# Two-layer hybrid block with routed experts: gate stores halved and doubled in number, part of them issued past the stage boundary, row products dealt out anew

## The chip, the cores and the metric

The kernel runs on one core of one Trainium2 chip. The metric is the time of one execution on the device, in microseconds, as the median of several executions. TensorE does the matrix products, VectorE, ScalarE and GpSimd the rest, and 16 DMA engines move data between the large memory (HBM) and the on-chip buffer (SBUF). The profile calls the engines PE, DVE, ACT and POOL; SP is the engine that only issues transfers.

## The reference, cut to what matters

Two layers, each of three parts: a mixer, an attention over a memory of 256 rows, and a feed-forward part with 16384 small experts. The change lies in the third, apart from the renaming of two semaphores. There, 512 tokens of width 1024 each choose 16 experts in each of 8 heads, 128 in all:

```python
idx = top 16 of the 16 x 16 sums of two top-16 lists, per head   # 8 heads
gate = softmax(best_v)
h = gelu(einsum('ted,td->te', expert_u[it], xt))
out = einsum('te,ted->td', gt * h, expert_v[it])
```

## The kernel before, in words

**Tiling of the expert part.** The 512 tokens are four tiles of 128 (token tile 0 to 3). Token tile 0 goes by gathered rows: for each of its 128 selections GpSimd fetches one expert row per token by an indirect transfer (128 x 1024 f32, 512 KiB), VectorE multiplies it with the token and sums it (`dots`, L1794), and in the last stage it fetches rows of the second expert table and adds them (`add_row`, L1928). Token tiles 1 to 3 (384 tokens) go densely, through all 128 blocks of 128 experts, and their gates are spread out into a dense table `gates` of 128 x 128 x 384 in HBM.

**First stage.** A loop over 128 slots j, one for each expert block. In a slot SP loads one weight tile of 512 KiB (L82, `load_tile`), ACT splits off its high half (L89) and DVE the low half (L95), PE does 24 matmuls of 128x384 (L116 to L118), ACT takes the gelu of them (L1677, `hidden`), and SP stores that result of 192 KiB (`keep`, L1516). Four f32 tiles (`wf`) and four split tiles (`wh`, `wl`) stand in rings of four. The split for slot j + 4 is what ACT does right after the gelu of slot j, and DVE right after that: the DVE part of slot j begins with the L95 of tile j + 4. The load of tile j + 7 is issued by SP right after the store of the hidden result of slot j.

Beside that run three identical rounds of 36 slots, one for each of token tiles 1 to 3, after 4 slots at the start: 20 slots of selection (`choose`, 16 calls over 20 slots, each with VectorE's top-16 instructions, every second one with a second search), 4 slots of picking, 4 slots in between, 8 slots of spreading (two `chunk` calls each; PE L1617/L1618, ACT L1715 copies them into the buffer `stage`). So spreading takes slots 32 to 39, 68 to 75 and 104 to 111. Slots 112 to 127 are the last stretch. The 128 row products of token tile 0 are dealt out over the slots by the planner `dots_of_slot`, in proportion to a room that `dots_by` estimates from `other_work`.

**Gate stores.** When a token tile is spread, `keep` stores its gates from `stage` to HBM (L1522), 8 stores of 1 MiB, one in each of the first 8 slots that follow (40 to 47, 76 to 83, 112 to 119), in runs of 512 bytes. In SP's program a store stands between the hidden store of slot j and the load of tile j + 7.

**Second stage.** Again 128 blocks: SP loads the expert's second tile (512 KiB) and reads the hidden result and the gates of that block (192 KiB each, L1533 and L1534), DVE multiplies them, ACT and DVE split the product, PE does 24 matmuls of 128x384 (L1635 to L1637). GpSimd gathers one row per block into `vrow`, which lies in the memory of `stage`, as does the sum `acc`. The start of this stage waits for the last gate store in three places: SP before its first block, GpSimd before the first gather (L1737), and DVE before it clears `acc` (L1935, L1936).

The order on each engine is the program order: every engine runs its own list, and semaphores tie them. SP's list and GpSimd's list hold their waits in order too. Of HBM transfers, those of SP form one queue (q1), the indirect ones of GpSimd another (q0).

Of the kernel before, what the change touches and what calls it, by code (L numbers as in the profile page):

```python
# [15 lines left out]
P = 128  # L16
D, SEQ, DEPTH = 1024, 512, 2
KT, NT = D // P, SEQ // P
# [8 lines left out]
EB = PK  # L27
# [22 lines left out]
RING = 4  # L50
# [344 lines left out]
def ssm_parameters(m, dve, step, par, v, c, cc, b, lag):  # L395

    nc = m.nc
    lr, li = par[:, PAR["lam_re"]], par[:, PAR["lam_im"]]
    TT, OP = nc.vector.tensor_tensor, ALU
    dve.wait_ge(m.ssm_trig, 1)  # L400
    step(TT(v.are, v.r, v.cos, OP.mult))
    step(TT(v.aim, v.r, v.sin, OP.mult))
    step(TT(v.r2, v.r, v.r, OP.mult))
    step(nc.vector.tensor_scalar(v.re, v.are, -1.0, None, OP.add))
    step(TT(v.t0, lr, lr, OP.mult))
    step(TT(v.t1, li, li, OP.mult))
    step(TT(v.t0, v.t0, v.t1, OP.add))
    step(nc.vector.reciprocal(v.inv, v.t0))
    step(TT(v.t0, v.re, lr, OP.mult))
    step(TT(v.t1, v.aim, li, OP.mult))  # L410
    step(TT(v.t0, v.t0, v.t1, OP.add))
    step(TT(v.fre, v.t0, v.inv, OP.mult))
    step(TT(v.t0, v.aim, lr, OP.mult))
    step(TT(v.t1, v.re, li, OP.mult))
    step(TT(v.t0, v.t0, v.t1, OP.subtract))
    step(TT(v.fim, v.t0, v.inv, OP.mult))
    dve.wait_ge(m.weights, 16 * N_SMALL)
    wide = [P, ST, 2 * SC]
    fre, fim = (x.unsqueeze(2).to_broadcast(wide) for x in (v.fre, v.fim))
    t = v.wide  # L420
    step(TT(t[:, 0], c[:, 0], fre, OP.mult))
    step(TT(t[:, 1], c[:, 1], fim, OP.mult))
    step(TT(cc[:, 0], t[:, 0], t[:, 1], OP.subtract))
    step(TT(t[:, 0], c[:, 0], fim, OP.mult))
    step(TT(t[:, 1], c[:, 1], fre, OP.mult))
    step(nc.vector.scalar_tensor_tensor(cc[:, 1], t[:, 0], -1.0, t[:, 1], OP.mult, OP.subtract))
    are, aim = (x.unsqueeze(2).to_broadcast(wide) for x in (v.are, v.aim))
    step(TT(t[:, 0], b[:, 0], are, OP.mult))
    step(TT(t[:, 1], b[:, 1], aim, OP.mult))
    step(TT(lag[:, 0], t[:, 0], t[:, 1], OP.subtract))  # L430
    step(TT(t[:, 0], b[:, 0], aim, OP.mult))
    step(TT(t[:, 1], b[:, 1], are, OP.mult))
    step(TT(lag[:, 1], t[:, 0], t[:, 1], OP.add))
    dve.sem_inc(m.lags, 1)
    step(TT(t[:, 0], cc[:, 0], are, OP.mult))
    step(TT(t[:, 1], cc[:, 1], aim, OP.mult))
    step(TT(cc[:, 2], t[:, 0], t[:, 1], OP.add))
    step(TT(t[:, 0], cc[:, 0], aim, OP.mult))
    step(TT(t[:, 1], cc[:, 1], are, OP.mult))
    step(TT(cc[:, 3], t[:, 1], t[:, 0], OP.subtract))  # L440
# [21 lines left out]
def mixer(nc, m, a, layer):  # L462
# [71 lines left out]
    def tensor(pe):  # L534
# [40 lines left out]
        for b in range(NT):  # L575
            pe.wait_ge(m.evac, N_IN + 6 + b - 1)
            MM(B[(N_IN + 6 + b) % 2][:, 0:MH * MV], ckv[:, 0, b * P:(b + 1) * P], ukv[:, MH * NOPE:],
               start=True, stop=True).then_inc(m.up, 1)
        pe.wait_ge(m.lags, 1)
        for z in range(2):  # L580
            pe.wait_ge(m.evac, N_IN + 10 + z - 1)
            for j in range(ST // 4):
# [4 lines left out]
        for st in range(ST):  # L587
            j, q = st // 4, st % 4
# [199 lines left out]
    def scalar(act):  # L788
# [38 lines left out]

        for i in range(13):
            if i == 6:
                act.wait_ge(m.keys_turned, 1)  # L830
                stick(0)
            act.wait_ge(m.up, i + 1)
            bank = B[(N_IN + i) % 2]
            if i < 6:
                for z in range(2):
                    last = AF((qh, kh)[i // 3][0:NOPE, 2 * (i % 3) + z, :], bank[64 * z:64 * z + 64, :], ACT.Copy)
            elif i < 10:
                last = AF(vm[:, i - 6, :], bank[:, 0:MH * MV], ACT.Copy)
            elif i < 12:
                last = AF(ab[:, i - 10], bank[:, 0:ST // 4 * P].rearrange("p (j n) -> p j n", j=ST // 4), ACT.Copy)  # L840
            else:
                last = AF(now, bank[:, 0:ST // 4 * 2 * SC].rearrange("p (j n) -> p j n", j=ST // 4), ACT.Copy)
            last.then_inc(m.evac, 1)
# [153 lines left out]
    def vector(dve):  # L997
        step = Steps(dve, m.dve_step)
        dve.sem_inc(m.split_done, 2 * RING)
        for n in range(N_IN):  # L1000
# [20 lines left out]
                STT(ml[:, :, :], memf, XS, mh[:, :, :], ALU.mult, ALU.subtract).then_inc(m.mem_low, 1)  # L1021
            if n == T_KRS + 8:
                ssm_parameters(m, dve, step, par, v, cz, cc, bs, lag)
        dve.sem_inc(m.keys_turned, 1)

        def turn_queries(r):
            dve.wait_ge(m.rot, r + 1)
# [370 lines left out]
R_PICK = 1  # L1398
# [1 line left out]
R_U = EB // RING  # L1400
ST_N = NT - 1
R_LAST = R_U - R_PICK - ST_N * R_TOK
STORES = 8
TURN = RING - 1
AHEAD = RING - 1
ND = SEQ - P
N_SEL = PH * TOP
GR = 4
HALF = TOP // 2
LATER = 2 * RING - 1  # L1410
LONG, SHORT = 4, 4
# [22 lines left out]
    return 1.3 + CPH * 2.8  # L1434


def dots_by(j):

    room = [min(1.8, max(0.0, 5.6 - other_work(i))) for i in range(EB)]
    return int(sum(room[:j]) * N_SEL / sum(room) + 0.5)  # L1440


# [5 lines left out]
def experts(nc, m, a, layer):  # L1448
# [57 lines left out]
    def sync(sp):  # L1506
        sp.wait_ge(m.mem_yl, KT)
        sp.dma_start(keys, a.keys[layer]).then_inc(m.keys_in, 16)
        with sp.Fori(0, R_PQ) as r:
            for k in range(RING):  # L1510
                load_tile(m, sp, a.proj[layer, r * RING + (T_PQ + k)], r + R_0, k)

        def keep(j):

            sp.wait_ge(m.tile_out, N_PQ + j + 1 + 2)
            sp.dma_start(m.hid[j], gst[j % RING]).then_inc(m.g_out[j % RING], 16)  # L1516
            for tt in range(1, NT):
                c = j - spread_slots(tt).stop
                if c in range(STORES):
                    i = slice(c * EB // STORES, (c + 1) * EB // STORES)  # L1520
                    sp.wait_ge(m.staged, tt * CPT + 2)
                    sp.dma_start(m.gates[i, :, (tt - 1) * P:tt * P].rearrange("i j t -> j i t"), stage[:, i, :])\  # L1522
                        .then_inc(m.gates_out, 16)

        for j in range(EB):
            if j >= LATER:
                keep(j - LATER)
            load_tile(m, sp, a.experts[layer, j], R_0 + R_PQ + j // RING, j % RING)

        def block(g, k):  # L1530
            load_tile(m, sp, a.experts[layer, g * RING + (EB + k)], g + (R_0 + R_PQ + R_U), k)
            sp.wait_ge(m.gw_used, g * RING + (k + 1))
            sp.dma_start(gw[:, k, 0, :], m.hid[g * RING + k]).then_inc(m.gw_in[k], 16)  # L1533
            sp.dma_start(gw[:, k, 1, :], m.gates[g * RING + k]).then_inc(m.gw_in[k], 16)  # L1534

        sp.wait_ge(m.gates_out, 16 * STORES * ST_N)
        for k in range(RING):
            sp.wait_ge(m.g_out[k], 16 * 2 + 1)
        for g in range(2):
            for k in range(RING):  # L1540
                if EB + g * RING + k - LATER < EB:
                    keep(EB + g * RING + k - LATER)
                block(g, k)
        for k in range(RING):
            sp.wait_ge(m.g_out[k], 16 * R_U + 1)
        with sp.Fori(2, R_U // 2) as g:
            for k in range(RING):
                block(g, k)
        sp.wait_ge(m.dots, N_SEL)
        sp.dma_start(m.xT[:, :, :], m.xsave.rearrange("p (k t) -> p k t", k=KT)).then_inc(m.x_back, 16)  # L1550
        with sp.Fori(R_U // 2, R_U) as g:
            for k in range(RING):
                block(g, k)
        for k in range(RING):
            load_tile(m, sp, a.tiles[layer * N_PROJ + (N_PROJ + k)], R_0 + R_PQ + 2 * R_U, k)
# [171 lines left out]
    def gpsimd(pool):  # L1727
# [3 lines left out]
        for i in range(N_SEL):  # L1731
            if i >= GR:
# [1 line left out]
            pool.indirect_dma_start(urow[:, i % GR, :], None, a.urows,  # L1734
                                    bass.IndirectOffsetOnAxis(ap=uidx[:, i:i + 1], axis=0))\
                .then_inc(m.u_in[i % GR], 16)
        pool.wait_ge(m.gates_out, 16 * STORES * ST_N)  # L1737
        rows = a.experts.rearrange("l e p d -> (l e p) d")
        for i in range(N_SEL):
            if i >= GR:  # L1740
# [6 lines left out]
    def vector(dve):  # L1747
# [184 lines left out]
            slot(j)  # L1932
            dots(j)
        step.restart()
        dve.wait_ge(m.gates_out, 16 * STORES * ST_N)  # L1935
        step(V.memset(acc, 0.0))  # L1936
        for k in range(RING):
            slot(EB - RING + k)
# [32 lines left out]


INPUTS = "x mem positions freq mask par proj experts urows keys uq ukv glu bz cz bs".split()
SEMAPHORES = """lags keys_turned split_done tile_used high_done params weights s_x s_small s_pool s_ang s_sin evac lat_sq lat_sum
lat_done up rot rot_done ssm_exp ssm_args ssm_trig table ssm_bu ssm_mul ssm_prod ssm_read
ssm_y sb_z sb_sp sb_t sb_w sb_wm sb_o sb_y mla_sc mla_nm mla_e mla_p mla_tr mla_pt mla_av mla_y
gelu_done glu_in glu_mm glu_sig glu_done grp_sq grp_sum y_norm yh_done yl_done
lat_sd grp_sd xh_done mem_in mem_high mem_low kv_out q_out mem_sc mem_nm mem_e mem_p mem_tr mem_pt mem_av
mem_yh mem_yl keys_in tile_out act_step dve_step pool_step scored
sc_copied best gate_e selected sel_turned sel_high hot spread  # L1980
staged gates_out gw_used multiplied prod_high prod_done out_done xtok_turned xtok_in idx_ready dots dots_gelu added
x_saved x_back second_hot""".split()


# [3 lines left out]
def program(nc, inputs, out, depth=DEPTH):  # L1988
    with ExitStack() as ctx:
        def sb(name, shape, dt=F32):  # L1990
# [7 lines left out]
        m = Named()  # L1998
        m.nc = nc
        sems = [ctx.enter_context(nc.semaphore(name)) for name in SEMAPHORES]  # L2000
        (m.lags, m.keys_turned, m.split_done, m.tile_used, m.high_done, m.params, m.weights, m.s_x, m.s_small, m.s_pool,
         m.s_ang, m.s_sin, m.evac, m.lat_sq, m.lat_sum, m.lat_done, m.up, m.rot, m.rot_done,
         m.ssm_exp, m.ssm_args, m.ssm_trig, m.table, m.ssm_bu, m.ssm_mul, m.ssm_prod, m.ssm_read,
         m.ssm_y, m.sb_z, m.sb_sp, m.sb_t, m.sb_w, m.sb_wm, m.sb_o, m.sb_y, m.mla_sc, m.mla_nm, m.mla_e,
# [2 lines left out]
         m.lat_sd, m.grp_sd, m.xh_done, m.mem_in, m.mem_high, m.mem_low, m.kv_out, m.q_out, m.mem_sc, m.mem_nm,  # L2007
         m.mem_e, m.mem_p, m.mem_tr, m.mem_pt, m.mem_av, m.mem_yh, m.mem_yl, m.keys_in, m.tile_out, m.act_step,
         m.dve_step, m.pool_step, m.scored, m.sc_copied, m.best, m.gate_e,
         m.selected, m.sel_turned, m.sel_high, m.hot, m.spread, m.staged, m.gates_out,  # L2010
         m.gw_used, m.multiplied, m.prod_high, m.prod_done, m.out_done, m.xtok_turned, m.xtok_in, m.idx_ready,
         m.dots, m.dots_gelu, m.added, m.x_saved, m.x_back, m.second_hot) = sems
        m.loaded = [ctx.enter_context(nc.semaphore(f"loaded{k}")) for k in range(RING)]
# [162 lines left out]
```

## Time and profile before

| what | value |
|---|---|
| time, median of 3 executions | 3841.4 us (3839.28 to 3844.2) |
| the profiled execution's own time | 3847.1 us |
| its span, first to last instruction | 3845.4 us |
| PE busy | 3446.5 us (90%) |
| DVE busy | 2873.0 us (75%) |
| ACT / POOL busy | 1480.1 us (38%) / 1020.2 us (27%) |
| mean granted TensorE clock | 0.954 |
| moved by DMA | 840.91 MB |

The expert part of layer 1 takes from about 705 us to about 1890 us of the span, that of layer 2 from about 2615 us. A row of the windows view gives, for one stretch, the busy time of each engine with its instructions, the granted clock of PE, the busy share of the DMA engines and the GB/s that they moved. A row of the waits view reads "engine, line, what it waited for: us in total, times, longest". A row of the timeline is start, duration, engine, line, operation, and in brackets the idle time before it with what ended it.

### The profile page before, as it was taken

To read this page: it belongs to the slowest core of one execution; us is meant where nothing else is said; L and a number is where in the kernel's file an instruction comes from. 1 tells how busy PE (TensorE), PEld (TensorE's weight loads), DVE (VectorE), ACT (ScalarE), POOL (GpSimd) and SP (SyncE) were. 2 spreads that over 40 slices of the span, in tenths; PEclk is the share of its full clock that TensorE was granted. 3 is DMA by queue.
4 is the path that set the end of the run, shared out by engine and by line. 5 is a ranking of instruction groups with operands and counts; after the bars stand their busy time and mean duration, and the time that the engine had idled before them with its cause. 6 is when DMAs were issued, how large, how long until landed. Compare 5 with 4: busy or idle time off the path is not lost.

```text
span 3845.4 us, 58583 instructions
## 1 busy us (share of the span) xinstructions
PE 3446.5 (90%) x20122; PEld 1992.1 (52%) x20122; DVE 2873.0 (75%) x5232; ACT 1480.1 (38%) x1978; POOL 1020.2 (27%) x742
## 2 busy tenths in 40 slices
PE   7899988979798889999888999889787979999997
PEld 3444644546464556666444446345454546566663
DVE  5765435898979768888847654368989896788887
ACT  4324423335353533333333244223343535333333
POOL 0510100231413134444324100002323141344442
PEclk9999998989999999999998899999998999999998
DMA  5001312586869699999540013126778786999995
GB/s 172 29 1 50 127 55 77 204 285 238 319 208 317 217 375 370 374 387 371 212 143 12 1 61 116 55 88 234 259 270 285 239 322 212 377 368 379 384 369 189
DMA packets 386162, 840.91 MB, mean 219 GB/s; under 512 B 32608, under 2 KB 231264, under 8 KB 385248
## 3 DMA queue, kind: packets, MB, share of 16 engines
q1 hardware_dynamic: 311712, 565.38, 42.0%
q0 software_dynamic: 73728, 268.47, 19.0%
q10 hardware_dynamic: 576, 5.37, 0.4%
q8 instruction: 60, 0.98, 0.1%
q14 instruction: 86, 0.70, 0.1%
HBM read 732.14 MB, written 106.95 MB: 218 GB/s over the span
## 4 chain that ended last, share of the span: by engine, by line
PE 31%; DVE 9%; DMA 3%; issue 3%; ACT 2%; SPq 2%; DVEq 0%; POOL 0%; ACTq 0%
PE ps L1635 4%; PE ps L1637 4%; PE ps L1636 4%; PE ps L116 3%; PE ps L117 3%; PE ps L118 3%; DMA wf<-experts 2%; SPq L82 2%; DVE wl L95 1%; DVE xT L1794 1%; DMA xT<-urows,small 1%; PE ps L152 1%; ACT wh L89 1%; ACT xh L181 0%; DVE small L1759 0%
## 5 line engine op out<-in xcount | busy, mean ns | idle before, releaser
L116 PE MATMUL ps<-xh,wh 128*128 128x384 f16 (+1 forms) x2880 | 1007.1, 350 | 215.2 <-DVE wl L95 62.9
L95 DVE SCALAR_TENSOR_TENSOR wl<-wf,wh 128x1024 f16<-128x1024 f32 x656 | 804.1, 1227 | 443.9 <-ACT wh L89 421.7
L89 ACT ACTIVATE wh<-wf 128x1024 f16<-128x1024 f32 x656 | 690.7, 1053 | 1025.2 <-PE ps L1637 582.3
L117 PE MATMUL ps<-xl,wh 128*128 128x384 f16 (+1 forms) x2880 | 1005.4, 349 | 0.0
L118 PE MATMUL ps<-xh,wl 128*128 128x384 f16 (+1 forms) x2880 | 1003.8, 349 | 0.0
L1734 POOL DMA_INDIRECT xT<-urows,small x256 | 363.4, 1419 | 1170.6 <-DVE xT L1794 888.6
L1635 PE MATMUL ps<-work,wh 128*128 128x384 f16 x2048 | 667.7, 326 | 6.0 <-DVE work L1919 4.3
L1637 PE MATMUL ps<-work,wl 128*128 128x384 f16 x2048 | 667.6, 326 | 0.0
L1636 PE MATMUL ps<-work,wh 128*128 128x384 f16 x2048 | 667.6, 326 | 0.0
L1742 POOL DMA_INDIRECT work<-experts,small x256 | 453.1, 1770 | 579.9 <-DVE work L1928 553.6
L116 PEld LDWEIGHTS ps<-xh,wh 128*128 128x128 f16 x2880 | 287.7, 100 | 478.0 <-ACT work L1677 104.5
L118 PEld LDWEIGHTS ps<-xh,wl 128*128 128x128 f16 x2880 | 287.7, 100 | 243.6 <-issue 20.9
L117 PEld LDWEIGHTS ps<-xl,wh 128*128 128x128 f16 x2880 | 287.5, 100 | 230.8 <-issue 19.2
L1928 DVE SCALAR_TENSOR_TENSOR work<-work,small 128x1024 f32<-128x1024 f32 x256 | 328.9, 1285 | 96.9 <-DVE work L1919 96.2
L1794 DVE SCALAR_TENSOR_TENSOR xT<-xT,work 128x1024 f32<-128x1024 f32 x256 | 308.2, 1222 | 19.8 <-DMA xT<-urows,small 12.5
L1635 PEld LDWEIGHTS ps<-work,wh 128*128 128x128 f16 x2048 | 200.4, 98 | 139.1 <-issue 5.0
L1637 PEld LDWEIGHTS ps<-work,wl 128*128 128x128 f16 x2048 | 200.4, 98 | 132.4
L1636 PEld LDWEIGHTS ps<-work,wh 128*128 128x128 f16 x2048 | 200.4, 98 | 131.4
L202 POOL TENSOR_SCALAR xT<-xT,small 128x512 f32<-128x512 f32 x24 | 51.9, 2171 | 748.2 <-ACT xh L181 748.2
L1677 ACT ACTIVATE work<-ps 128x384 f32<-128x384 f32 x192 | 93.5, 487 | 326.7 <-PE ps L118 300.9
L1715 ACT ACTIVATE work<-ps 128x1024 f32<-128x1024 f32 x96 | 184.0, 2011 | 51.6 <-PE ps L1618 51.6
L1617 PE MATMUL ps<-work,sq 128*128 128x128 f16 x768 | 114.7, 239 | 62.5 <-DVE sq L1885 62.5
(347 smaller groups left out, 4146.2 us busy)
## 6 DMA issues: line engine op xcount, KB each, us to landing
wf<-experts SPq DMA_DIRECT2D x512, 512.0 KB
wf<-proj SPq DMA_DIRECT2D x144, 512.0 KB
gates<-work SPq DMA_DIRECT2D x48, 1024.0 KB
work<-hid SPq DMA_DIRECT2D x256, 192.0 KB
work<-gates SPq DMA_DIRECT2D x256, 192.0 KB
hid<-work SPq DMA_DIRECT2D x192, 192.0 KB
hid<-small SPq DMA_DIRECT2D x64, 192.0 KB
xsave<-xT ACTq DMA_DIRECT2D x2, 2048.0 KB, 7.0
```

The source lines that it names most:

```text
L89: m.nc.scalar.activation(m.wh[:, slot, :], m.wf[:, k, :], ACT.Copy, scale=WS).then_inc(m.high_done, 1)
L95: m.nc.vector.scalar_tensor_tensor(m.wl[:, slot, :], m.wf[:, k, :], WS, m.wh[:, slot, :], ALU.mult, ALU.subtract).then_inc(m.split_done, 1)
L116: m.nc.tensor.matmul(out, wh[:, k, :], xh[:, k, 0:n], start=(k == order[0]), stop=False)
L117: m.nc.tensor.matmul(out, wh[:, k, :], xl[:, k, 0:n], start=False, stop=False)
L118: last = m.nc.tensor.matmul(out, wl[:, k, :], xh[:, k, 0:n], start=False, stop=(k == order[-1]))
L1635: MM(out, m.wh[:, k, c], ph[:, k, :], start=first, stop=False)
L1636: MM(out, m.wh[:, k, c], pl[:, k, :], start=False, stop=False)
L1637: done = MM(out, m.wl[:, k, c], ph[:, k, :], start=False, stop=last)
L1734: pool.indirect_dma_start(urow[:, i % GR, :], None, a.urows, bass.IndirectOffsetOnAxis(ap=uidx[:, i:i + 1], axis=0))\
L1742: pool.indirect_dma_start(vrow[:, i % GR, :], None, rows, bass.IndirectOffsetOnAxis(ap=vidx[:, i:i + 1], axis=0))\
L1794: STT(row, row, 1.0, xtok, ALU.mult, ALU.mult, accum_out=hd[:, i:i + 1]).then_inc(m.dots, 1)
L1928: STT(acc, row, wd[:, bass.ds(i, 1)], acc, ALU.mult, ALU.add).then_inc(m.added, 1)
```

## The change

- `STORES` is 16 in place of 8: each gate store has 512 KiB (8 of the 128 first-key columns), one in each of the 16 slots after a spreading.
- `HEAD` is 5, the number of stores that free the memory of `vrow` and `acc`. The first five stores of the last token tile count on a semaphore of their own, `gates_head`.
- `keep` runs seven slots behind SP's loads, so that the last seven stores of the last token tile now stand in SP's program among the first blocks of the second stage. SP waits there for the two earlier token tiles and for the five; it waits for all stores before its third group of four blocks. GpSimd and DVE wait for the five alone.
- The planner `dots_by` gives a storing slot a room of at most 1.1, any other at most 1.9 (1.8 before for all).
- Two semaphores, `lags` and `keys_turned`, become one, `prepared`, waited for at 1 and at 2. DVE raises them in that order before and after.

```diff
-    dve.sem_inc(m.lags, 1)
+    dve.sem_inc(m.prepared, 1)
...
-        pe.wait_ge(m.lags, 1)
+        pe.wait_ge(m.prepared, 1)
...
-                act.wait_ge(m.keys_turned, 1)
+                act.wait_ge(m.prepared, 2)
...
-        dve.sem_inc(m.keys_turned, 1)
+        dve.sem_inc(m.prepared, 1)
...
-STORES = 8
+GR = 4
+STORES = 16
+HEAD = -(-STORES * (GR + 1) * D // (EB * P))
...
+def storing(j):
+
+    at = j - R_PICK * RING
+    return at >= R_TOK * RING and at % (R_TOK * RING) < STORES
...
-    room = [min(1.8, max(0.0, 5.6 - other_work(i))) for i in range(EB)]
+    room = [min(1.1 if storing(i) else 1.9, max(0.0, 5.6 - other_work(i))) for i in range(EB)]
...
+                    done = m.gates_head if tt == NT - 1 and c < HEAD else m.gates_out
                     sp.dma_start(m.gates[i, :, (tt - 1) * P:tt * P].rearrange("i j t -> j i t"), stage[:, i, :])\
-                        .then_inc(m.gates_out, 16)
+                        .then_inc(done, 16)
...
-        sp.wait_ge(m.gates_out, 16 * STORES * ST_N)
+        sp.wait_ge(m.gates_out, 16 * STORES * (ST_N - 1))
+        sp.wait_ge(m.gates_head, 16 * HEAD)
         for k in range(RING):
             sp.wait_ge(m.g_out[k], 16 * 2 + 1)
         for g in range(2):
...
                 block(g, k)
+        sp.wait_ge(m.gates_out, 16 * (STORES * ST_N - HEAD))
         for k in range(RING):
             sp.wait_ge(m.g_out[k], 16 * R_U + 1)
...
-        pool.wait_ge(m.gates_out, 16 * STORES * ST_N)
+        pool.wait_ge(m.gates_head, 16 * HEAD)
...
-        dve.wait_ge(m.gates_out, 16 * STORES * ST_N)
+        dve.wait_ge(m.gates_head, 16 * HEAD)
```

Worked out from the two formulas, the planner deals the 128 row products of a layer so:

| slots | what else is there | products before | products after |
|---|---|---|---|
| 0 to 31 | selection, picking | 35 | 44 |
| 32 to 39, 68 to 75, 104 to 111 | spreading | 0 | 0 |
| 40 to 55 | selection; stores | 22 | 16 |
| 56 to 67 | selection, picking | 17 | 20 |
| 76 to 91 | selection; stores | 21 | 16 |
| 92 to 103 | selection, picking | 17 | 20 |
| 112 to 127 | stores | 16 | 12 |

## Rows read from the trace of the kernel before

**Rows 1.** Page: busy time and share of each engine; DMA share in 40 slices.
```profile
PE 3446.5 (90%) x20122; PEld 1992.1 (52%) x20122; DVE 2873.0 (75%) x5232; ACT 1480.1 (38%) x1978; POOL 1020.2 (27%) x742
...
DMA  5001312586869699999540013126778786999995
```

**Rows 2.** Windows, layer 1: stretch, its us, busy per engine, clock, DMA share, GB/s.
```profile
730.00:912.00 182.00, 158.33 (x1074) 99.23 (x1072) 167.09 (x389) 81.80 (x91) 52.29 (x36) 0.94 0.71 246
912.00:998.00 86.00, 73.50 (x432) 42.14 (x431) 74.01 (x217) 26.91 (x37) 30.33 (x21) 0.97 1.00 353
998.00:1069.00 71.00, 54.03 (x321) 31.99 (x320) 64.65 (x136) 23.18 (x31) 25.46 (x19) 0.84 0.78 274
...
1113.00:1200.00 87.00, 75.02 (x433) 42.86 (x431) 72.55 (x215) 26.53 (x37) 27.68 (x20) 0.94 1.01 346
...
1313.00:1391.00 78.00, 62.84 (x365) 36.04 (x364) 37.98 (x51) 22.68 (x34) 19.34 (x16) 0.96 1.02 350
1391.00:1850.00 459.00, 459.00 (x2827) 276.37 (x2825) 402.19 (x474) 174.46 (x238) 206.21 (x116) 1.00 1.01 376
```

**Rows 3.** Waits of DVE from 912 to 998 us (layer 1, first stores).
```profile
DVE wl L95 <- ACT wh L89: 12.0, 4, 4.9
DVE wl L95 <- issue: 1.3, 1, 1.3
```

**Rows 4.** The same from 1113 to 1200 us (layer 1, second stores).
```profile
DVE wl L95 <- ACT wh L89: 16.0, 5, 5.5
```

**Rows 5.** The same from 2824 to 2909 us (layer 2, first stores).
```profile
DVE wl L95 <- ACT wh L89: 13.5, 5, 4.8
```

**Rows 6.** The same from 3025 to 3110 us (layer 2, second stores).
```profile
DVE wl L95 <- ACT wh L89: 13.8, 5, 4.8
DVE wl L95 <- issue: 0.8, 1, 0.8
```

**Rows 7.** Waits of DVE from 998 to 1069 us (between stores).
```profile
DVE xT L1794 <- DMA xT<-urows,small: 2.3, 3, 1.4
```

**Rows 8.** Waits of ACT from 912 to 998 us.
```profile
ACT wh L89 <- DMA wf<-experts: 36.0, 11, 7.0
```

**Rows 9.** Waits of ACT from 1313 to 1391 us (last stretch).
```profile
ACT wh L89 <- DMA wf<-experts: 44.3, 10, 7.1
```

**Rows 10.** Timeline of DVE, slots 43 to 46, selection with stores.
```profile
926.55 1.22 DVE L95 SCALAR_TENSOR_TENSOR wl<-wf,wh 128x1024 f16<-128x1024 f32 x1
...
929.38 1.23 DVE L1794 SCALAR_TENSOR_TENSOR xT<-xT,work 128x1024 f32<-128x1024 f32 x1
...
930.53 1.22 DVE L1794 SCALAR_TENSOR_TENSOR xT<-xT,work 128x1024 f32<-128x1024 f32 x1
...
931.68 1.22 DVE L95 SCALAR_TENSOR_TENSOR wl<-wf,wh 128x1024 f16<-128x1024 f32 x1
...
937.67 1.22 DVE L95 SCALAR_TENSOR_TENSOR wl<-wf,wh 128x1024 f16<-128x1024 f32 x1
...
943.57 1.23 DVE L95 SCALAR_TENSOR_TENSOR wl<-wf,wh 128x1024 f16<-128x1024 f32 x1 [2.39 <-ACT wh L89]
```

**Rows 11.** Timeline of DVE: where its slots 40 and 56 begin.
```profile
912.67 1.22 DVE L95 SCALAR_TENSOR_TENSOR wl<-wf,wh 128x1024 f16<-128x1024 f32 x1 [4.87 <-ACT wh L89]
...
997.53 1.22 DVE L95 SCALAR_TENSOR_TENSOR wl<-wf,wh 128x1024 f16<-128x1024 f32 x1
```

**Rows 12.** Timeline of ACT: the gelus of slots 112, 113 and 127.
```profile
1313.17 0.49 ACT L1677 ACTIVATE work<-ps 128x384 f32<-128x384 f32 x1 [0.88 <-PE ps L118]
...
1317.07 0.49 ACT L1677 ACTIVATE small<-ps 128x384 f32<-128x384 f32 x1 [2.46 <-PE ps L118]
...
1390.99 0.47 ACT L1677 ACTIVATE work<-ps 128x384 f32<-128x384 f32 x1
```

**Rows 13.** Timeline of SP: a load issued behind a gate store, slot 114.
```profile
1326.78 8.70 SPq L82 DMA_DIRECT2D wf<-experts  x1
```

**Rows 14.** Timeline of POOL: the first row gather of the second stage.
```profile
1373.40 0.94 POOL L1742 DMA_INDIRECT work<-experts,small  x1 [8.22 <-DMA gates<-work]
```

More of the change, by code:

```diff
@@ L1407 @@
 N_SEL = PH * TOP
-GR = 4
 HALF = TOP // 2
@@ L1973 @@
 INPUTS = "x mem positions freq mask par proj experts urows keys uq ukv glu bz cz bs".split()
-SEMAPHORES = """lags keys_turned split_done tile_used high_done params weights s_x s_small s_pool s_ang s_sin evac lat_sq lat_sum
+SEMAPHORES = """prepared split_done tile_used high_done params weights s_x s_small s_pool s_ang s_sin evac lat_sq lat_sum
 lat_done up rot rot_done ssm_exp ssm_args ssm_trig table ssm_bu ssm_mul ssm_prod ssm_read
@@ L1980 @@
 sc_copied best gate_e selected sel_turned sel_high hot spread
-staged gates_out gw_used multiplied prod_high prod_done out_done xtok_turned xtok_in idx_ready dots dots_gelu added
+staged gates_out gates_head gw_used multiplied prod_high prod_done out_done xtok_turned xtok_in idx_ready dots dots_gelu added
 x_saved x_back second_hot""".split()
@@ L2000, in program @@
         sems = [ctx.enter_context(nc.semaphore(name)) for name in SEMAPHORES]
-        (m.lags, m.keys_turned, m.split_done, m.tile_used, m.high_done, m.params, m.weights, m.s_x, m.s_small, m.s_pool,
+        (m.prepared, m.split_done, m.tile_used, m.high_done, m.params, m.weights, m.s_x, m.s_small, m.s_pool,
          m.s_ang, m.s_sin, m.evac, m.lat_sq, m.lat_sum, m.lat_done, m.up, m.rot, m.rot_done,
@@ L2009, in program @@
          m.dve_step, m.pool_step, m.scored, m.sc_copied, m.best, m.gate_e,
-         m.selected, m.sel_turned, m.sel_high, m.hot, m.spread, m.staged, m.gates_out,
+         m.selected, m.sel_turned, m.sel_high, m.hot, m.spread, m.staged, m.gates_out, m.gates_head,
          m.gw_used, m.multiplied, m.prod_high, m.prod_done, m.out_done, m.xtok_turned, m.xtok_in, m.idx_ready,
```

## The prediction
> **What bounds the kernel now.** I read the page first: PE is busy 90% of the span and DVE 75%, and the DMA share swings between 0 and 9 tenths [rows 1]. No engine bounds the whole, so I cut the expert part of layer 1 by the windows view at the places where the work changes [rows 2]. Three kinds of stretch show.
>
> Selection and spreading without stores (730 to 912 us, 998 to 1069): DVE is busy 167.09 of 182 us and 64.65 of 71, PE is not full, DMA is at 0.71 and 0.78. The waits of DVE there sum to 2.3 us in 71 [rows 7]; what else is missing are gaps of a tenth between dependent instructions. DVE is the bound, and PE waits for it.
>
> Selection with stores (912 to 998, 1113 to 1200): DMA is at 1.00 and 1.01, and DVE, which should be the bound here too, stands idle [rows 3 to 6]. It waits for ACT's split, and ACT for the weight tile: 36.0 us in 11 waits [rows 8]. A gate store of 1 MiB stands in the queue ahead of each tile's load; SP needs 8.70 us to hand over one such load, since the queue ahead of it is full [rows 13].
>
> The last stretch (1313 to 1391): DVE is busy 37.98 of 78 us, DMA at 1.02, and ACT waits 44.3 us for tiles [rows 2, 9]. Here DMA alone bounds. From 1391 on PE is busy 459 of 459 us at clock 1.00: PE bounds the second stage, with DMA at 1.01 and 376 GB/s right behind [rows 2].
>
> **Prices.** One row product costs DVE 1.15 us, from start to start (929.38 to 930.53) [rows 10]. A split costs 1.15 us too (937.67 to the next product; its row has 1.22 with the overlap). A slot with two products and a light `choose` takes 926.55 to 931.68 = 5.13 us, with one product and a heavy one 931.68 to 937.67 = 5.99 us [rows 10]. So a slot with one product takes DVE 2.3 us without `choose`, 3.98 with a light and 5.99 with a heavy one. PE's slot is 1317.07 - 1313.17 = 3.90 us [rows 12]. All sums are against the profiled execution's own 3847.1 us, which is 5.7 above the median of 3841.4.
>
> **A. Nine more products before slot 32.** That stretch is DVE's, so each costs in full: 9 x 1.15 x 2 layers = +20.7 us. From below, DVE idles some 2 us at its start while no product is there yet; I give nothing for it.
>
> **B. The storing slots of token tiles 1 and 2 (four regions).** Before, DVE goes from slot 40 at 912.67 to slot 56 at 997.53, 84.9 us [rows 11]. Of the 16 slots 4 have no `choose`, 6 a light, 6 a heavy one: with one product each, 4 x 2.3 + 6 x 3.98 + 6 x 5.99 = 69.0 us. Before, there are six more products, 6.9 us; 75.9 us are work, and 8.4 us are waits: 12.0 + 1.3 less the 4.9 that ended as slot 40 began, which belongs to the spreading [rows 3, 11]. The other regions have the same 4.9 or so at their start, so 16.0 - 4.9 = 11.1, 13.5 - 4.9 = 8.6 and 14.6 - 4.9 = 9.7 [rows 4 to 6]. Together 37.8 us of waits that DVE could lose.
>
> Does the queue keep up when each of 16 slots has a store of 512 KiB? The old window of 86 us at 353 GB/s moved 30.4 MB [rows 2]. Six gathered rows fewer are 3.1 MB. The rings hold three weight tiles and four rows when the stores begin, and these may run down by slot 56, 3.7 MB. That leaves 23.6 MB, at the same 353 GB/s 67 us, under DVE's 69.0. By the middle of the region only half the stores have been issued, where before all had been. So DVE bounds, not DMA, though by two or three us. Slot 40 now has a product less than PE's pace covers: DVE's 2.3 us against 3.90 leave 1.6 us idle. I add 1.0 us for tiles that come late, and so leave 4 x 2.6 = 10.4 of the 37.8. Gain 27.4. The products dealt away are 6 + 5 in each layer, 22 x 1.15 = 25.3. B is -52.7 us. Bounds: all waits stay but the products go, -25.3; all but the 1.6 go, -56.7.
>
> **C. Three more products in each of slots 56 to 67 and 92 to 103.** DVE's again: 12 x 1.15 = +13.8 us. With 2, 2, 1, 2 products in the slots before spreading the row gathers come closer together; the waits for a row were 2.3 us there [rows 7]. I add 1.5 us a layer, +3 (bounds 0 and +8).
>
> **D. The last stretch and the boundary.** From the gelu of slot 112 to that of slot 127 take 77.8 us [rows 12]. PE's floor is 15 x 3.90 = 58.5, plus up to one slot at the end, 62.4. The old window moved 78 x 350 = 27.3 MB [rows 2]. Four gathered rows fewer are 2.1 MB. `keep` issues a store with each slot, so only the last four of sixteen are issued behind the load of the last tile that slot 127 needs (it was issued with slot 123): 2.1 MB more go behind the boundary. 23.1 MB at 350 GB/s are 66 us, a gain of 12; I take 10 a layer, -20, since a full queue also delays the rows. Bounds: 0 (the queue is just as full) and -15.4 (PE's floor).
>
> The waits that go: GpSimd's first gather waited 8.22 us for the last gate store [rows 14], SP and DVE behind it. It now starts once five stores have landed, which they have by about slot 118. Four rows of 2.1 MB then come some 8 us earlier; that moves traffic and saves no time by itself. What is late next is the tile behind them.
>
> The waits that are added: SP's wait for all stores before its third group. Behind it stand the loads and reads of blocks 8 on. The last store is issued two blocks before it, and PE at that time has split tiles for some three blocks, 11.7 us. In SP's first seven blocks a store stands ahead of each load; but SP reaches them when the gelus of slots 121 to 127 are done, at the pace of before, and the last four stores are all that PE's second stage sees. They are 2.1 MB, 5.6 us of the queue at 376 GB/s [rows 2], against those 11.7 us of reserve. I put their cost at 0 (bounds 0 and +5.6 a layer; inside D).
>
> The Trainium skill's "DMA: Bandwidth & Descriptors" (Bandwidth) gives about 358 GB/s as what HBM yields to one core. By that, the second stage would have been over its limit already and the 2.1 MB would come on top in full, 5.9 us a layer. The trace has 376 GB/s over 459 us with PE never idle [rows 2], and so decides against it.
>
> **E. The merged semaphore and more issues.** DVE raises `prepared` in the order in which both were raised, and PE and ACT wait at the same places: 0. Twenty-four more stores a layer cost SP half a microsecond each; SP waits far more than that: 0.
>
> Sum: +20.7 - 52.7 + 13.8 + 3 - 20 = -35.2 us. 3847.1 - 35.2 = 3811.9; less the 5.7, about **3806 us**.
>
> **The rivals.**
>
> R1, the queue is the bound of the storing slots still. The bytes of a region don't change but for the rows: then DVE's waits stay 37.8 and B is its lower bound, -25.3 in place of -52.7. For it: DMA at 1.00 through the region [rows 2]. Against: 67 against 69 us. Time 3806 + 27.4 = 3833. Chance 0.13.
>
> R2, the last stretch gains nothing: the row gathers of the second stage, now earlier, and the reads of hidden and gates take what the rows leave. D is 0: 3826. Chance 0.12.
>
> R3, slower. A store of half the size holds the queue for more than half the time, and it now stands ahead of 16 loads and not 8. The place is SP's list in slots 40 to 55 and 76 to 91; what shows it is SP's 8.70 us for one load behind a store [rows 13]. If DVE's storing region stays at about 85 us though it has six products less (5.3 us a slot in place of 4.4), B is 0, and with A, C and D the sum is +17.5: 3859. It decides from 81 us (5.1 a slot) on, where B is -17.5. Against it: the stores are cut in the same runs of 512 bytes, only fewer of them. Chance 0.07.
>
> "DMA: Bandwidth & Descriptors" of the Trainium skill has a rule that speaks for this rival (Bandwidth: batch transfers to 1 MiB or more; each carries some 2 us of fixed cost). By it the 48 additional stores would cost up to 96 us if nothing hid them, an estimate from that page. No row of before has a store of 512 KiB; its loads of that size keep 376 GB/s in the second stage, since many are under way [rows 2].
>
> **How the numbers follow.** My forecast has 0.68, R1 0.13, R2 0.12, R3 0.07. The forecast's own range is 3790 (all bounds at their good end but one) to 3820. R2 and most of R1 come in by 3832; left out is R3 with the tails. 0.2% is 7.7 us, about what a measurement of this kernel tells from no change: 3833.7 to 3849.1. Forecast and R2 are faster, R1 splits at the line. Faster 0.86, same 0.07, slower 0.07.
>
> **What would show it.** A: DVE's slot 32 begins some 10 us later. B: from slot 40 to 56 about 72 us where 84.9 were, DVE's waits for ACT under 3 us inside. C: the two stretches 3.5 us longer each. D: from gelu 112 to 127 about 67 us and PE without a gap after. I am wrong if DVE's waits in the storing slots stay above 6 us each (R1), if the last stretch stays over 75 us (R2), or if PE pauses after the boundary.

## The result, and the profile after

The changed kernel takes 3794.6 us (median of 4 executions, 3783.65 to 3811.34) where the kernel before takes 3842.8 in the same set of executions: a ratio of 0.9876, 95% interval 0.9835 to 0.9917. Five further executions of the same kernel gave 3795.9 (ratio 0.9865, 0.9844 to 0.9886). The forecast was 3806 with a range of 3790 to 3820; it had the sign and the place. The gain it foresaw was 35.2 us, the measured one is 48.2: 13 us short.

The profiled execution of the changed kernel is its fastest, 3783.65 us, so 63.4 us under the profiled one of before. The expert parts explain 50.3 of these: from the gelu of slot 0 to that of slot 127 they take 660.6 and 661.2 us where it was 685.8 and 686.2. The second stage is as long as before (in layer 1 500.4 us from that gelu to the start of its last matmul, now 500.8). The other 13 us lie in the mixer and the attention, where no line differs, most of them between the layers: 714.9 us there in place of 724.0. Over the twelve traces of this study that stretch takes 714 to 729 us, whatever the expert part does. It makes the scatter of the medians, and no effect of the change is read from it.

The page of after, first busy times, then the DMA share in slices; beside [rows 1] no slice changes by more than a tenth, so that the windows have to tell:

```profile
PE 3411.8 (90%) x20122; PEld 1982.1 (52%) x20122; DVE 2866.9 (76%) x5232; ACT 1482.0 (39%) x1978; POOL 1015.6 (27%) x742
...
DMA  5001312586969699999640013126869696999995
```

The windows of layer 1 that answer to [rows 2] (columns as there):

```profile
731.00:920.00 189.00, 157.92 (x1053) 98.17 (x1052) 173.98 (x395) 81.72 (x89) 64.61 (x44) 0.92 0.73 254
920.00:992.00 72.00, 70.78 (x436) 42.42 (x435) 67.20 (x205) 25.00 (x35) 24.93 (x16) 1.00 1.06 377
992.00:1069.00 77.00, 53.15 (x333) 32.23 (x331) 69.74 (x145) 27.26 (x35) 29.96 (x21) 0.87 0.80 282
1111.00:1183.00 72.00, 70.79 (x437) 42.41 (x436) 67.23 (x205) 25.49 (x36) 24.89 (x16) 1.00 1.06 378
1300.00:1363.00 63.00, 61.18 (x376) 36.51 (x375) 33.31 (x43) 22.73 (x33) 11.70 (x12) 1.00 1.03 367
1363.00:1820.00 457.00, 455.73 (x2801) 273.47 (x2800) 398.87 (x471) 173.84 (x237) 200.35 (x115) 1.00 1.01 380
```

The storing slots (second and fourth row) fell from some 86 to 72 us, with PE and DVE both nearly full and the queue at 377 GB/s instead of 353. The last stretch fell from 78 to 63. The granted TensorE clock rose from 0.97 and 0.96 in these windows [rows 2] to 1.00. In the storing slots DVE sets the pace; in the last stretch no run separates what the clock gave from what the shorter waits gave.

Where DVE's slots 40 and 56 begin, against [rows 11]:

```profile
920.31 1.23 DVE L95 SCALAR_TENSOR_TENSOR wl<-wf,wh 128x1024 f16<-128x1024 f32 x1 [4.88 <-ACT wh L89]
...
991.15 1.22 DVE L95 SCALAR_TENSOR_TENSOR wl<-wf,wh 128x1024 f16<-128x1024 f32 x1
```

That is 70.84 us. Its waits from 920 to 992 us, against [rows 3], and the row that answers to [rows 7], from 992 to 1069:

```profile
DVE wl L95 <- ACT wh L89: 6.4, 2, 4.9
...
DVE xT L1804 <- DMA xT<-urows,small: 3.7, 2, 3.5
```

4.9 of the 6.4 end as slot 40 begins; 1.5 are left. All four storing regions have the very same row. ACT's waits for tiles from 920 to 992 us and from 1300 to 1363, against [rows 8, 9]:

```profile
ACT wh L89 <- DMA wf<-experts: 15.8, 7, 3.7
```
```profile
ACT wh L89 <- DMA wf<-experts: 17.7, 7, 6.8
```

ACT still waits 15.8 us for tiles, and DVE hardly waits for ACT any more: it is busy with selection and has its tile when it comes to it. The gelus of slots 112 and 127, against [rows 12] (62.80 us), and GpSimd's last gather of the first and first of the second stage, against [rows 14]:

```profile
1300.36 0.49 ACT L1687 ACTIVATE work<-ps 128x384 f32<-128x384 f32 x1 [0.87 <-PE ps L118]
...
1363.16 0.47 ACT L1687 ACTIVATE work<-ps 128x384 f32<-128x384 f32 x1
```
```profile
1331.94 0.94 POOL L1744 DMA_INDIRECT xT<-urows,small  x1 [3.14 <-DVE xT L1804]
1333.18 0.94 POOL L1752 DMA_INDIRECT work<-experts,small  x1 [0.30 <-issue]
```

SP in the last stretch: a store and the load behind it as in [rows 13], here of slot 117, and the last store, between blocks of the second stage:

```profile
1321.29 0.72 SPq L1530 DMA_DIRECT2D gates<-work  x1
1322.20 3.27 SPq L82 DMA_DIRECT2D wf<-experts  x1
...
1370.15 0.44 SPq L1530 DMA_DIRECT2D gates<-work  x1
1370.77 2.00 SPq L82 DMA_DIRECT2D wf<-experts  x1
...
1378.06 0.34 SPq L82 DMA_DIRECT2D wf<-experts  x1
```

No load of this last stretch needs more than 5.07 us to be handed over, where one took 8.70. The load at 1378.06 is the first behind the new wait for all stores: 3.1 us after SP's last transfer before it.

### The profile page after: what moved, and what is told of

Its sections match the earlier page's. It is cut to its first block and busy times, and to the rows that moved or that the text cites. A ratio compares the mean times of both kernels' runs of the same rounds, so it can differ in the third digit from the quotient of the medians.

```text
span 3781.9 us, 58627 instructions
## 1 busy us (share of the span) xinstructions
PE 3411.8 (90%) x20122; PEld 1982.1 (52%) x20122; DVE 2866.9 (76%) x5232; ACT 1482.0 (39%) x1978; POOL 1015.6 (27%) x742
## 5 line engine op out<-in xcount | busy, mean ns | idle before, releaser
L95 DVE SCALAR_TENSOR_TENSOR wl<-wf,wh 128x1024 f16<-128x1024 f32 x656 | 803.7, 1226 | 393.8 <-ACT wh L89 378.4
L1752 POOL DMA_INDIRECT work<-experts,small x256 | 441.3, 1724 | 600.3 <-DVE work L1938 590.8
L117 PEld LDWEIGHTS ps<-xl,wh 128*128 128x128 f16 x2880 | 285.8, 99 | 229.8 <-issue 14.6
L1725 ACT ACTIVATE work<-ps 128x1024 f32<-128x1024 f32 x96 | 184.0, 2011 | 68.2 <-PE ps L1628 68.2
```

Of the source, the lines that this page charges most:

```text
L95: m.nc.vector.scalar_tensor_tensor(m.wl[:, slot, :], m.wf[:, k, :], WS, m.wh[:, slot, :], ALU.mult, ALU.subtract).then_inc(m.split_done, 1)
L117: m.nc.tensor.matmul(out, wh[:, k, :], xl[:, k, 0:n], start=False, stop=False)
L1752: pool.indirect_dma_start(vrow[:, i % GR, :], None, rows, bass.IndirectOffsetOnAxis(ap=vidx[:, i:i + 1], axis=0))\
```

## The experiments

All are set against the kernel before or the changed one. They ran in three sets after the first one, each with the kernel before beside it (its medians there 3845.0, 3843.5 and 3843.5 us), and each ratio is to that neighbour; so medians of different sets compare only to some 2 us. This table has, from each trace, DVE's way from slot 40 to 56 and from 76 to 92 (start of L95 to start of L95), the last stretch (gelu 112 to gelu 127), each for layer 1 / layer 2, and the first stage from gelu 0 to gelu 127.

| kernel | median, us | slots 40-56 | slots 76-92 | last stretch | first stage |
|---|---|---|---|---|---|
| before | 3842.8 | 84.9 / 85.2 | 86.5 / 85.3 | 77.8 / 77.2 | 685.8 / 686.2 |
| changed | 3794.6 | 70.8 / 70.8 | 70.8 / 70.8 | 62.8 / 62.6 | 660.6 / 661.2 |
| planner_only | 3852.4 | 82.2 / 82.3 | 80.2 / 80.9 | 70.4 / 70.5 | 692.7 / 690.5 |
| stores_only | 3797.2 | 76.6 / 76.6 | 76.5 / 76.5 | 67.5 / 68.2 | 655.9 / 659.8 |
| last_tile_as_before | 3811.5 | 70.9 / 70.9 | 70.9 / 73.4 | 69.5 / 70.0 | 668.1 / 673.3 |
| two_per_slot | 3856.1 | 79.2 / 79.2 | 79.2 / 78.9 | 75.0 / 72.6 | 694.2 / 687.4 |
| spread_end | 3784.3 | 70.0 / 70.7 | 69.7 / 69.7 | 65.3 / 65.2 | 650.7 / 655.9 |
| spread_end_more | 3785.7 | 69.2 / 67.9 | 67.4 / 72.9 | 63.5 / 65.1 | 649.4 / 657.0 |
| gathers_wait_for_all | 3808.4 | 70.8 / 70.8 | 70.8 / 70.8 | 58.5 / 59.3 | 660.6 / 658.2 |
| spread_end_16 | 3780.8 | 71.5 / 72.6 | 71.9 / 71.9 | 66.6 / 66.9 | 648.6 / 654.3 |
| last_tile_8_early_start | 3819.0 | 70.8 / 70.8 | 70.8 / 70.8 | 74.8 / 72.2 | 674.5 / 671.1 |

### planner_only: the new deal of row products in the kernel before

```diff
-    room = [min(1.8, max(0.0, 5.6 - other_work(i))) for i in range(EB)]
+    room = [min(1.1 if storing(i) else 1.9, max(0.0, 5.6 - other_work(i))) for i in range(EB)]
```

> The kernel before with the new deal of row products alone (16, 16, 12 in the storing slots, 44, 20, 20 elsewhere), stores of 1 MiB in eight slots and all waits as before. Theory (VectorE bounds outside the stores, the gain comes from tiles that are no longer late there): from slot 40 to 56 VectorE has 69.0 us of work, but the tiles are as late in the eight crowded slots as before, so about 78 us with 8 us of waits; +22 us before slot 32 and +18 in the slots between, -28 in the four storing regions, -11 in the two last stretches: about the time of before, 3835 to 3850. Rival (the new deal is what brings the gain, since it takes 15 rows a layer off a full queue): storing regions near 71 us, in all 3810 or less.

Measured 3852.4 us, ratio 1.0019 (1.0005 to 1.0032): a little slower than before. The deal alone saves nothing. DVE's waits in the storing slots grew as its work shrank; from 925 to 1008 us:

```profile
DVE wl L95 <- ACT wh L89: 17.2, 7, 4.9
```

12.3 us of waits after the first 4.9, where 8.4 were. Six products fewer are 6.9 us less work, but this region falls by 2.7 only; all four fall by 16.2 us for 25.3 us less work, and the two last stretches by 14.1. The slots before 32 and those between pay 23.5 and 20.3 for it. The rival (3810 or less) falls; the theory had the waits too low (8 us, and 78 us for a region that took 80 to 82).

### stores_only: the changed kernel with the old deal

```diff
-    room = [min(1.1 if storing(i) else 1.9, max(0.0, 5.6 - other_work(i))) for i in range(EB)]
+    room = [min(1.8, max(0.0, 5.6 - other_work(i))) for i in range(EB)]
```

> The changed kernel with the deal of row products of before (22, 21, 16 in the storing slots). Theory: the 512 KiB stores alone take the waits away; slot 40 to 56 has 75.9 us of VectorE work and takes about 78, 76 to 92 about 77, the last stretch 66 us since four more rows pass the queue; against before -7 and -9 a region and -11 a last stretch, about -54 in all: 3785 to 3800, the same as the changed kernel. Rival (the deal brings the gain): storing regions stay at 82 us or more with over 5 us of waits each, time 3815 or more.

Measured 3797.2 us, ratio 0.9878 (0.9858 to 0.9899): not told apart from the changed kernel. With 22 products the storing slots take 76.6 us, and DVE waits (913 to 990 us) hardly at all:

```profile
DVE wl L95 <- ACT wh L89: 5.2, 2, 4.8
```
```profile
913.00:990.00 77.00, 70.54 (x431) 41.67 (x429) 73.66 (x217) 23.63 (x34) 31.84 (x21) 1.00 1.05 379
```

So the queue carries sixteen stores of 512 KiB and 22 rows within DVE's own time: it had more room than I had given it. The four storing regions are 35.6 us shorter than before with the same products, of 37.8 us of waits that there were to lose. The gain is that of the stores and their waits; the new deal only moves DVE's work about. The first stages of stores_only are even 1 to 5 us shorter than those of the changed kernel.

### two_per_slot: sixteen stores of 512 KiB, crowded into eight slots

```diff
-                c = j - spread_slots(tt).stop
-                if c in range(STORES):
+                at = j - spread_slots(tt).stop
+                for c in (2 * at, 2 * at + 1):
+                    if c not in range(STORES):
+                        continue
```

> The changed kernel, but the sixteen stores of 512 KiB are issued two per slot in the first eight slots after each spreading. Theory (it is the spread over 16 slots that counts, not the size): storing regions about 78 us with 7 to 8 us of waits, last stretch 70 to 72 us, in all as the kernel with the new deal alone, 3835 to 3850. Rival (small transfers leave gaps in the queue, so that loads pass sooner): regions stay near 71 us and the time near 3795. Rival (each transfer has a fixed price): slower than the new deal alone by some 2 us for each of 48 stores.

Measured 3856.1 us, ratio 1.0025 (1.0011 to 1.0040). The whole gain of the stores is gone: the four storing regions are shorter than before by 25.4 us, just the 25.3 us of products dealt away, and the last stretches are 2 to 5 us longer than with the new deal alone. DVE's waits from 931 to 1011 us:

```profile
DVE wl L95 <- ACT wh L89: 14.2, 7, 4.8
```

What counts is how the bytes of the stores are spread over the loads. The number of transfers does not: this kernel has 48 stores more than planner_only and storing regions 1 to 3 us shorter, and its last stretches (75.0 / 72.6) are those of eight stores of 1 MiB in the same eight slots with the same early start (74.8 / 72.2, last_tile_8_early_start below). The Trainium skill's "DMA: Bandwidth & Descriptors" (Anatomy of one DMA — SWDGE (gpsimd) path) gives a fixed cost of some 2 us for each transfer issued by GpSimd. Nothing of the kind shows in these stores, which SP issues and of which many are under way.

One kernel was not tried: eight stores of 1 MiB, one in every second slot. So it is not shown whether the stores had to be halved, or only to be spread over 16 slots.

### last_tile_as_before: the last stretch undone

```diff
+                n = 8 if tt == NT - 1 else STORES
...
-        sp.wait_ge(m.gates_out, 16 * STORES * (ST_N - 1))
-        sp.wait_ge(m.gates_head, 16 * HEAD)
+        sp.wait_ge(m.gates_out, 16 * (STORES * (ST_N - 1) + 8))
...
-        pool.wait_ge(m.gates_head, 16 * HEAD)
+        pool.wait_ge(m.gates_out, 16 * (STORES * (ST_N - 1) + 8))
```

> The changed kernel, but the last token tile goes out in 8 stores of 1 MiB within the first stage, and SP, GpSimd and VectorE wait for all of them at the boundary. Theory: the two earlier regions stay at 70.8 us; the last stretch goes from 62.7 back to about 72 us (77.5 less four rows of 1.4 us), +18 to +20 in all: about 3813. Rival (the last stretch gained only by its four fewer products and by the earlier gathers of the second stage): 65 to 68 us, under +10.

Measured 3811.5 us, ratio 0.9917 (0.9888 to 0.9946), 17 over the changed kernel. The last stretch takes 69.5 and 70.0 us, 2 us less than the theory had: 7 us a layer are the last tile's stores and waits. That planner_only has 70.4 and 70.5 says that the four rows fewer make the other 7 of the 15.

### last_tile_8_early_start: eight stores, but the early start

```diff
# last_tile_as_before, but with the waits of the changed kernel on the first three stores
-                    done = m.gates_head if tt == NT - 1 and c < HEAD else m.gates_out
+                    done = m.gates_head if tt == NT - 1 and c < 3 else m.gates_out
```

> The last token tile in eight stores of 1 MiB as in last_tile_as_before, but with the changed kernel's waits: the second stage starts after the three stores that free the memory of the rows. Theory (in the last stretch it is the spreading of the stores over 16 slots that gained, 7 us a layer; with eight stores all are issued by slot 119 and the first gathers are early anyway): last stretch 69 to 70 us, 3810. Rival (the early start at the boundary gained it): last stretch 65 us or less, 3800 or less.

Measured 3819.0 us, ratio 0.9939 (0.9926 to 0.9953): 23 over the changed kernel. The intervals of this ratio and of last_tile_as_before overlap; that the early start made it slower is read from the last stretch, 74.8 and 72.2 us where 69.5 and 70.0 were. The rival falls; the theory's 69 to 70 us were too low by 3 to 5. ACT's waits for tiles from 1309 to 1384 us:

```profile
ACT wh L89 <- DMA wf<-experts: 32.4, 7, 9.6
```

GpSimd's four gathers now start at 1352.3 us, amid what the eight stores have queued, and one tile comes 9.6 us late; with the late start the longest such wait is 5.2. So the early start costs 2 to 5 us a layer where the stores are crowded.

### gathers_wait_for_all: only GpSimd's start undone

```diff
+        pool.wait_ge(m.gates_out, 16 * (STORES * ST_N - HEAD))
         pool.wait_ge(m.gates_head, 16 * HEAD)
```

> The changed kernel, but GpSimd waits for all gate stores before its first gather of the second stage. Theory (the earlier gathers move traffic and save no time by themselves; the last stretch gains by the stores being spread out): last stretch 60 to 63 us, and the time within 4 us of the changed kernel. Rival (the gain of the last stretch is that of the early gathers): it goes back to 68 us or PE pauses after the boundary, +7 a layer and more.

Measured 3808.4 us, ratio 0.9905 (0.9888 to 0.9921), 12.5 over the changed kernel. The theory was wrong, and its rival right in one half: PE pauses after the boundary. The last stretch does not go back to 68 us; it is shorter than the 60 to 63 expected. Without the four rows it runs at PE's pace without a break in layer 1, 58.5 us, just 15 x 3.90, and takes 59.3 in layer 2. But the last store now lands late, and the first gather with it; the waits of DVE and of PE from 1385 to 1410 us:

```profile
DVE work L1939 <- DMA work<-experts,small: 11.3, 1, 11.3
```
```profile
PE ps L1645 <- DVE work L1930: 9.4, 1, 9.4
```

DVE stands 11.3 us before the first row, and PE behind it. The second stage takes 512.7 and 512.4 us in place of 500.8 and 500.6. The later row start costs 12 us a layer there and gives back 3 to 4 in the last stretch.

### after_again, spread_end, spread_end_more, spread_end_16: a better deal

> The changed kernel itself, unaltered, as the measure for the three that follow on the same chip: 3795, and the storing regions at 70.8 us with 1.5 us of waits.

Measured 3795.9 us; storing regions 70.8 to 70.9. Its first stages take 662.1 and 661.6 us: two traces of one kernel differ there by up to 1.5 us.

The deal of spread_end:

```diff
-    return int(sum(room[:j]) * N_SEL / sum(room) + 0.5)
+    ends = 4 * sum(i < j for i in (39, 75, 111))
+    return ends + int(sum(room[:j]) * (N_SEL - 12) / sum(room) + 0.5)
```

> The changed kernel with four of the row products in each last spreading slot (39, 75, 111), and the other 116 dealt out as by the changed planner. VectorE stood idle 4.8 to 4.9 us before slot 40, 76 and 112 in every trace, and four rows lie ready there. Theory (outside the last stretch a product costs 1.15 us wherever VectorE has work, and nothing where it waits): eleven products a layer leave stretches where they cost, -12.7 us a layer, and the spreading stays at 52 us: about 25 us under the changed kernel. Rival (four gathers start together with the first stores, and the queue becomes the bound): the storing regions rise from about 68.5 to 73 us, gain under 10.

Measured 3784.3 us, ratio 0.9837 (0.9816 to 0.9858): 11.6 under the changed kernel, not 25. The four products at 915.40 to 919.98 us fill the gap and the spreading stays at 52 us:

```profile
915.40 1.22 DVE L1805 SCALAR_TENSOR_TENSOR xT<-xT,work 128x1024 f32<-128x1024 f32 x1
...
918.84 1.22 DVE L1805 SCALAR_TENSOR_TENSOR xT<-xT,work 128x1024 f32<-128x1024 f32 x1
...
920.35 1.23 DVE L95 SCALAR_TENSOR_TENSOR wl<-wf,wh 128x1024 f16<-128x1024 f32 x1 [0.29 <-ACT wh L89]
```

So they are free, but four of the twelve came out of slots 40 to 55 and 76 to 91, which fell by 0.2 to 1.1 us each for them and not by 2.3, and the last stretch grew by 2.5 and 2.7. The rival's dearer storing slots did not come; its gain, under 10, was nearer to the 11.6 than the theory's 25. The first stages are 11.4 and 5.7 us shorter than in after_again; the intervals of the two ratios overlap at their ends.

What spread_end_more adds to it:

```diff
+    ends += sum(i < j for s in (32, 68, 104) for i in (s + 2, s + 4, s + 6))
+    return ends + int(sum(room[:j]) * (N_SEL - 21) / sum(room) + 0.5)
```

> As spread_end, with one further product in each of slots 34, 36, 38, 70, 72, 74, 106, 108, 110, where VectorE waits 0.75 us in the slot after. Theory: each costs 1.15 less 0.75 there and saves 1.15 elsewhere, nine a layer, another 7 us a layer or 14 in all. Rival (in the spreading the chain PE, ScalarE, VectorE bounds, and a product delays it in full): nothing further, or slower by up to 5 us.

Measured 3785.7 us, ratio 0.9853 (0.9833 to 0.9873). A spreading with three products more takes 55.1 to 56.3 us where it took 51.3 to 53.0: about 1.1 us for each, what it saves elsewhere. The rival was right.

The deal of spread_end_16, against the changed kernel:

```diff
-    return int(sum(room[:j]) * N_SEL / sum(room) + 0.5)
+    rest = [0.0 if storing(i) else r for i, r in enumerate(room)]
+    fixed = sum(storing(i) and i < EB - RING for i in range(j)) + 4 * sum(i < j for i in (39, 75, 111))
+    return fixed + int(sum(rest[:j]) * (N_SEL - 44 - 12) / sum(rest) + 0.5)
```

> As spread_end (four products in each last spreading slot), but each storing slot keeps its one product (16, 16, 12), and all twelve are taken from the slots between (37, 18 and 17 in place of 44, 20 and 20). In spread_end five of its twelve came out of storing slots. Theory (in a storing slot a product below one saves nothing, since there the pace of TensorE and the tiles bound): storing regions 71 to 72 us, and 12 x 1.15 = 13.8 us a layer saved elsewhere against the changed kernel, less 2 us for rows that come late after slot 39: 20 to 24 us under the changed kernel, 3772 to 3776. Rival (the queue is full at the start of the stores, and sixteen rows more behind four gathers at once make tiles late): storing regions 74 us, no better than spread_end, 3784.

Measured 3780.8 us, ratio 0.9843 (0.9828 to 0.9857), 15 under the changed kernel, where 20 to 24 were expected, and the lowest median of the study. Its interval overlaps that of spread_end, and its first stages are 2.1 and 1.6 us shorter, hardly more than two traces of one kernel differ; so no order of these two is shown. The storing slots take 71.5 to 72.6 us, near the 71 to 72 expected. What was not expected is the last stretch, 66.6 and 66.9. The four rows used in slot 111 have to be fetched anew amid the stores, where the queue bounds; that this is the cause is argued, not tried.

## Why the prediction was right, and where it was short

**What bounds.** Right. DVE bounded all but the storing slots and the last stretch; stores_only shows that the waits there were what could be gained, planner_only that taking products out does not bring it.

**A**, nine products more before slot 32: forecast +20.7 us over both layers, measured 10.5 + 11.6 = +22.1 from DVE's slot 6 to 32.

**B**, the storing slots: forecast -52.7, measured from 341.8 us in all four to 283.4, -58.5, just beyond its bound of -56.7. The work was 69.0 as counted, plus the 1.6 us of PE's pace in slot 40: 70.6 forecast without late tiles, 70.84 measured. The 1.0 us a region that I added for late tiles did not come. R1 rested on the queue's room, for which I had 67 against 69 us. That sum had two terms wrong, and they made up for one another; so that DVE bounded "by two or three us" was in part luck. The first is the rate. 353 GB/s was the mean of a window in which the queue was not full throughout; the DMA view of the kernel before from 912 to 998 us has the share in tenths and the GB/s in 40 slices of 2.15 us:

```profile
DMA  7999999999999999999999999999999999599935
GB/s 203 283 211 371 384 393 401 380 363 309 353 407 372 400 387 385 401 396 378 370 392 348 399 349 381 415 415 418 417 409 423 406 402 426 177 326 295 320 139 122
```

In its last six slices the stores are long out, and it has caught up. The window without them, 912 to 985 us, has 375 GB/s, as the queue carried 377 to 379 in the two kernels with the new stores. The second term is the bytes. I took 3.7 MB off for the rings to run down, and 23.6 were left; the window of after moved 72 x 377 = 27.1 MB, the 30.4 less the 3.1 of six rows. At 353 GB/s 27.1 MB would have been 77 us, above DVE's 69.0. How much of it those slots needed, no run tells.

**C**, the slots between: forecast 13.8 + 3, measured +18.5. DVE's gaps in these stretches were 1.5 to 3.1 us and are now 1.5 to 5.2.

**D**, the last stretch: forecast -20, measured -15.0 and -14.6, -29.6. This is the largest miss, and here the bytes were right and the rate was not: I had 23.1 MB to move, and the window of after moved 63 x 367 = 23.1 MB. At 350 GB/s that made 66 us, at 367 it makes 63. The 350 had no slack in it (share 1.02); the rate itself is another with the stores spread out, which nothing in the old trace told. Beyond that I had taken 10 for 12 us. PE's floor, 62.4 in the prediction, is 58.5 (gathers_wait_for_all). The four early rows are the 3 to 4 us between.

**The waits.** That the earlier start of the gathers "saves no time by itself" was wrong as a reading of the code: the deferred stores make it necessary, 12 us of the second stage hang on it. Nor is it 8 us earlier: from the gelu of slot 112 the first gather was 60.2 us away and is now 32.8, so 27 us earlier. As a term of the sum it did no harm, since the change has both. The wait that was added cost nothing to be seen: PE's second stage is 500.8 us with the stores inside, it is busy 455.73 of its first 457 us, and SP's first load behind the wait comes 3.1 us after its last transfer, against the 11.7 us of reserve that I had counted on. That 2.1 MB more at the boundary cost nothing agrees with 380 GB/s over 457 us. The 358 GB/s of the Trainium skill ("DMA: Bandwidth & Descriptors", Bandwidth) is what that section gives each core with both cores of a pair streaming; I had left that out. For a core alone, as here, its table goes up to 425; the trace, with 380, stays within that.

**E**, semaphore and issues: nothing seen; the merged semaphore was not tried alone.

The spreadings fell by 2.8 us in all, for which no term stood. Sum of the expert parts: -50.3 where -35.2 was forecast. The profiled execution is 28 us under the 3811.9 forecast for it: 15 of these are in the expert parts, 13 in the parts that did not change.

## What to carry to other kernels

Where a bulk store and a just-in-time load share one queue, count how long the load stands behind the store, not only the bytes: the same bytes in twice as many stores, one ahead of each load, took 48 us off, the part past the stage boundary included, and the same stores issued in pairs gave all of it back. When a transfer is deferred past a stage boundary, look for what waits for it on other engines and split the wait; here 12 us a layer hung on that. And take a queue's rate only from a window in which it is full throughout: a mean that included the slack at its end, 353 for 375 GB/s, made the storing slots too dear by 6%. Even a rate without slack holds only for its own pattern: 350 GB/s in the last stretch became 367.

## What was not expected of the hardware

A full queue does not have one rate, even with the same kinds of transfer in it. In windows whose mean share is 1.0 or more it moved 350 GB/s in the last stretch of before [rows 2] and 360 in that of two_per_slot, both with the stores crowded; 367 in that of the changed kernel, with the stores spread out; and 377 and 378 in its storing slots. The second stage has 376 before and 380 after. Crowding is not all of it: gathers_wait_for_all, with the stores spread, moved 361 from 1310 to 1369 us at a share of 1.02, and PE never waited there. So a share of 1.0 does not say either that the queue could carry no more. What sets the rate stays open.
